# Triangular inversions of a decoder kernel: the value product on four corners of the array instead of two

## The chip, the cores and the metric

The kernel runs on one core of a Trainium2 chip. The core has TensorE (matrix products, PE in the profile, with its weight loads as PEld), VectorE (DVE), ScalarE (ACT), GpSimd (POOL) and SyncE (SP), which issues the transfers. The metric is the device time of one execution in microseconds (us); lower is better.

## The reference, cut to what matters

Two decoder layers over 256 tokens of width 1024. Each layer mixes three branches (RWKV-7, gated DeltaNet, sparse latent attention), adds a cross attention over 256 memory tokens, and ends in a feed-forward part (dense in layer 0, top 2 of 8 experts in layer 1). Two of the branches are recurrences over tokens that a chunked kernel turns into the inverse of a unit triangular matrix for each head and chunk of 64 tokens:

```python
    # gated DeltaNet, for each of 8 heads and 4 chunks of C = 64 tokens
    Lmat = jnp.where(strict, jnp.einsum('bhnid,bhnjd->bhnij', kb, k) * decay, 0.0)
    rhs = jnp.concatenate([v * beta, kb * jnp.exp(g)[..., None]], axis=-1)
    sol = lax.linalg.triangular_solve(Lmat + jnp.eye(C, dtype=jnp.float32), rhs,
                                      left_side=True, lower=True, unit_diagonal=True)
    ...
    # RWKV-7, for each of 16 heads, one token after another
    def step(S, inp):
        r_t, w_t, k_t, v_t, kk_t, a_t = inp
        sa = jnp.einsum('bhvk,bhk->bhv', S, -kk_t)
        S = (S * w_t[:, :, None, :] + sa[..., None] * (kk_t * a_t)[:, :, None, :]
             + v_t[..., None] * k_t[:, :, None, :])
        return S, jnp.einsum('bhvk,bhk->bhv', S, r_t)
```

All of this is computed in float32.

## The kernel before

Every engine has a program of its own, written as Python generators that are interleaved by hand; what an engine does next is fixed by the place of each `yield`, and the engines meet at semaphores (`wait_ge`, `then_inc`, and a `Counter` that keeps the numbers).

**The inversion.** `invert` (TensorE), and the two functions called `inverted` (one for ScalarE, one for VectorE) compute unit triangular inverses by doubling: 6 levels (`LEVELS`), block size 1, 2, 4 up to 32. One call treats two *sets*, i = 0 and 1; a set is eight 64x64 matrices, four (q = 0 to 3) on partitions 0 to 63 and four on partitions 64 to 127 (`HALF`). For each level and set:

- **F** (L765): TensorE adds 8 products of 64x64 by 64 columns into columns 0 to 255 of bank 2 + i. The last level has none.
- **W** (L2223): VectorE multiplies that bank with the mask of the next level into `w`, an operand of the next F and V.
- **V** (L770): TensorE adds 8 products of 64x64 by 128 columns (64 at the last level) into bank 4 + i, which then holds, side by side, the matrix and the inverse so far.
- **VU** (L1596): ScalarE copies the whole bank 4 + i (128x512) into `vu`, the other operand of the next F and V.

Every product of a matrix on partitions 0 to 63 also has its result on partitions 0 to 63, and in the same way for the other half: of the four 64x64 corners of the array, the two on the diagonal are used. A product in float32 stands in the profile as two LDWEIGHTS and two MATMUL rows, so 8 products are "x16". At the end of a call ScalarE copies the inverses to `xt_` (L1602). Ahead of the levels, TensorE writes F's start (L748), and V's start as a product with the identity (L753) and two with the corner identity (L755) for each set.

**What lies around it.** An inversion is called 12 times, 6 in each layer. `filled` on TensorE puts one *dense unit* (two products of 128x256 at L799, a quarter of a projection tile) behind each of the `yield`s in `invert`, and, where the yielded value is true, one step of a second generator. In this text the calls have letters:

- **B** (first and third in each layer, `rw_set(i, i)`): RWKV, beside the *front* of the next two pairs of heads (`front_rw`). The front is a chain over three engines: on TensorE two low-rank products (L859, L860), then two sums (L865, L867), then the Gram products (L875, L876); on ScalarE two copies and a square, four sigmoids and a table load (L1650 to L1665), later a logarithm and exponentials; on VectorE four stretches, the first (from L2248) ending at L2257, behind the sigmoids.
- **A** (second and fourth, `rw_set(i, 2 + i)`): RWKV, beside dense units alone.
- **G1** (fifth): gated DeltaNet with `corners` (it also joins the 64-blocks to 128), beside `front_gd` of four heads, three steps to a head. `both` advances this front at every yield.
- **G2** (sixth): the same, beside the first recurrence, `recur_gd(0)`, and dense units.

The order of each engine's queue is that of its own generators: what ScalarE and VectorE do for the front stands in line with VU and W.

Of the kernel before, what the change touches and what calls it, by code (L numbers as in the profile page):

```python
# [14 lines left out]
P = 128  # L15
# [130 lines left out]
def build(nc, x, mem, consts, params, w_in, w2, a2, v1, v2, w_uq, w_uk, w_uv, w_qI, w_mix, xa_q, xa_kv, xa_o,  # L146
          ff_g, ff_u, ff_d, router, me_g, me_u, me_d, final_norm, v_first, out):
    ctx = ExitStack()
    with ctx:
# [89 lines left out]
        HALF = (slice(0, 64), slice(64, P))  # L239

# [395 lines left out]
        def _(pe):  # L636
# [100 lines left out]
            def invert(sets, corners=None):  # L737
# [12 lines left out]
                for i, (nt, xt_, vu, w) in enumerate(sets):  # L750
                    if corners is not None:
                        pe.wait_ge(S["inv_VU"], c.need("inv_VU"))
                    mm(bk4(4 + i)[:, :, 64:P], C("ident"), b4(C("eye2")), start=True, stop=True, skip_group_check=True)  # L753
                    for h, p_ in enumerate(HALF):
                        m = mm(bk4(4 + i)[p_, :, 0:64], C("eye2")[p_], nt[h], start=False, stop=True, skip_group_check=True)  # L755
                    m.then_inc(S["inv_V"], 1)
                for b in range(LEVELS):
                    last = b == LEVELS - 1
                    for i, (nt, xt_, vu, w) in enumerate(sets):
                        pe.wait_ge(S["inv_W"], c.need("inv_W"))  # L760
# [771 lines left out]
        def _(act):  # L1532
# [52 lines left out]
            def inverted(sets, corners=False):  # L1585
# [6 lines left out]
                for b in range(LEVELS):  # L1592
                    for i, (nt, xt_, vu, w) in enumerate(sets):
                        act.wait_ge(S["inv_V"], c.need("inv_V"))
                        act.wait_ge(*c.last())
                        sc.activation(vu, bk4(4 + i), ACT.Copy).then_inc(*c.inc("inv_VU"))  # L1596
                        yield i
                for i, (nt, xt_, vu, w) in enumerate(sets):
                    act.wait_ge(S["inv_V"], c.need("inv_V"))
                    for h, p_ in enumerate(HALF):  # L1600
                        act.wait_ge(*c.last())
                        sc.activation(xt_[p_, :, p_], bk4(4 + i)[p_, :, 64:P], ACT.Copy).then_inc(*c.inc("inv_XT" if h else "act_step"))  # L1602
                if corners:
                    yield 0
                    for i in range(len(sets)):
                        act.wait_ge(S["inv_V"], c.need("inv_V"))
                        act.wait_ge(*c.last())
                        sc.activation(gB[0:64, i, 1], bk(4 + i, 0, T)[0:64].rearrange("p (a b) -> p a b", a=4), ACT.Copy).then_inc(*c.inc("inv_VU"))
                    yield 1
# [535 lines left out]
        def _(dve):  # L2145
# [72 lines left out]
            def inverted(sets, corners=False):  # L2218
                q4 = lambda ap: ap.rearrange("p (a b) -> p a b", a=4)
                for b in range(LEVELS):  # L2220
                    for i, (nt, xt_, vu, w) in enumerate(sets):
# [3 lines left out]
                        yield i  # L2225
# [637 lines left out]
```

## Time and profile before

| | |
|---|---|
| time, median of 3 runs | 2955.32 us (2954.4 to 2958.49) |
| span of the profiled execution | 2958.0 us |
| TensorE busy in it | 2588.5 us, 88% |
| ScalarE busy | 1469.3 us, 50% |
| VectorE busy | 1706.3 us, 58% |
| mean granted TensorE clock | 0.954 |
| the 12 inversion calls together | 561.67 us, TensorE busy 487.99 us |

The span runs from the first to the last instruction. No separate time is listed for the profiled execution; its span lies within the range of the three runs, 2.7 us above their median, so no time of note lies around it. Busy times are of each engine for itself and overlap. In the rows below a timeline row gives start, duration (from the start of the first to the end of the last of the merged instructions), engine, line, operation, tiles and count, and in brackets how long the engine had been idle and who ended that.

### The profile page before, as it was taken

To read this page: it belongs to the slowest core of one execution; us is meant where nothing else is said; L and a number is where in the kernel's file an instruction comes from. 1 tells how busy PE (TensorE), PEld (TensorE's weight loads), DVE (VectorE), ACT (ScalarE), POOL (GpSimd) and SP (SyncE) were. 2 spreads that over 40 slices of the span, in tenths; PEclk is the share of its full clock that TensorE was granted. 3 is DMA by queue.
4 is the path that set the end of the run, shared out by engine and by line. 5 is a ranking of instruction groups with operands and counts; after the bars stand their busy time and mean duration, and the time that the engine had idled before them with its cause. 6 is when DMAs were issued, how large, how long until landed. Compare 5 with 4: busy or idle time off the path is not lost.

```text
span 2958.0 us, 67158 instructions
## 1 busy us (share of the span) xinstructions
PE 2588.5 (88%) x29799; PEld 2117.4 (72%) x29818; DVE 1706.3 (58%) x1983; ACT 1469.3 (50%) x1911; POOL 358.2 (12%) x180
## 2 busy tenths in 40 slices
PE   7988988899797989897988999787898898998986
PEld 6766666777465768665666777557888888888875
DVE  2445463234215542545462233128999999999996
ACT  2233343233224331433343233137888889888885
POOL 0000001000000000000001000001323243324231
PEclk9999999999998999998989999898999999999999
DMA  6411120123216634301121133237999999999994
GB/s 201 135 41 47 31 86 29 37 93 114 95 62 228 202 119 139 100 30 31 58 63 32 58 107 100 100 125 289 388 386 386 386 386 388 382 386 390 385 387 183
DMA packets 304032, 531.34 MB, mean 180 GB/s; under 512 B 18528, under 2 KB 145760, under 8 KB 303360
## 3 DMA queue, kind: packets, MB, share of 16 engines
q1 hardware_dynamic: 303600, 525.99, 50.3%
q8 instruction: 236, 3.87, 0.5%
q10 hardware_dynamic: 144, 1.05, 0.1%
q14 instruction: 52, 0.43, 0.0%
HBM read 524.91 MB, written 2.10 MB: 178 GB/s over the span
## 4 chain that ended last, share of the span: by engine, by line
PE 53%; DVE 33%; ACT 7%; issue 6%; DMA 0%; ACTq 0%; DVEq 0%; SPq 0%
DVE arena L2713 24%; PE bank L799 11%; PE bank L700 9%; PE bank L770 4%; PE bank L1277 4%; PE bank L1236 4%; PE bank L765 3%; PE bank L718 2%; DVE yacc L2721 2%; PE bank L1293 2%; PE bank L644 2%; PE bank L1025 1%; ACT arena L1897 1%; PE bank L875 1%; PE bank L1030 1%
## 5 line engine op out<-in xcount | busy, mean ns | idle before, releaser
L2713 DVE TENSOR_TENSOR arena<-ring,arena 128x2048 bf16<-128x2048 f32 x336 | 833.4, 2525 | 3.8 <-ACT arena L2012 3.8
L2012 ACT ACTIVATE arena<-ring 128x2048 bf16<-128x2048 f32 x336 | 640.4, 1911 | 98.9 <-DMA ring<-in_moe_w_down 30.2
L1378 PE MATMUL bank<-arena 128*128 128x0 bf16 x10752 | 490.6, 209 | 99.4 <-DVE arena L2713 96.3
L1378 PEld LDWEIGHTS bank<-arena 128*128 128x128 bf16 x10752 | 478.6, 100 | 113.7 <-DVE arena L2713 105.3
L799 PE MATMUL bank<-feat,ring 128*128 128x256 f32 x1664 | 433.6, 399 | 8.4 <-ACT ring L1575 2.3
L1527 POOL TENSOR_TENSOR arena<-yacc,arena 128x512 bf16<-128x512 f32 x112 | 300.2, 2692 | 1004.5 <-ACT arena L2035 1004.5
L799 PEld LDWEIGHTS bank<-feat,ring 128*128 128x128 f32 x1664 | 308.6, 196 | 87.3 <-issue 43.1
L1395 PEld LDWEIGHTS bank<-arena 128*128 128x128 bf16 x5376 | 237.8, 98 | 23.0 <-issue 20.0
L1395 PE MATMUL bank<-arena 128*128 128x0 bf16 x5376 | 245.0, 206 | 7.3 <-issue 3.8
L700 PE MATMUL bank<-feat,ring 128*128 128x256 f32 x1056 | 236.8, 388 | 7.7 <-issue 5.7
L700 PEld LDWEIGHTS bank<-feat,ring 128*128 128x128 f32 x1056 | 205.7, 195 | 38.2 <-ACT feat L1566 8.9
L1504 POOL TENSOR_TENSOR arena<-arena 64x512 f32<-64x512 f32 x16 | 23.1, 1443 | 1152.1 <-ACT arena L1677 971.8
L1582 ACT ACTIVATE arena<-bank 128x256 f32<-128x256 f32 x120 | 46.1, 384 | 189.3 <-PE bank L700 91.2
L644 PE MATMUL bank<-cs,arena 128*128 128x128 f32 (+1 forms) x424 | 71.0, 304 | 69.3 <-ACT arena L1558 40.4
L1277 PE MATMUL bank<-arena 128*128 128x256 bf16 x1056 | 119.7, 276 | 10.6 <-DVE arena L2610 10.6
L2223 DVE TENSOR_TENSOR arena<-bank,cs 128x256 f32<-128x256 f32 x144 | 61.1, 424 | 117.5 <-PE bank L765 70.9
L1277 PEld LDWEIGHTS bank<-arena 128*128 128x128 bf16 x1056 | 104.5, 99 | 26.4 <-issue 11.0
L644 PEld LDWEIGHTS bank<-cs,arena 128*128 128x128 f32 (+1 forms) x424 | 53.8, 157 | 83.1 <-issue 29.2
L770 PE MATMUL bank<-arena 64*64 64x128 f32 (+1 forms) x1536 | 102.7, 276 | 6.6 <-ACT arena L1596 4.2
L765 PEld LDWEIGHTS bank<-arena 64*64 64x64 f32 x1280 | 47.4, 140 | 83.2 <-issue 43.6
L765 PE MATMUL bank<-arena 64*64 64x64 f32 x1280 | 56.4, 229 | 56.9 <-ACT arena L1596 32.5
L1582 ACT ACTIVATE ring<-bank 128x256 f32<-128x256 f32 x50 | 19.2, 384 | 153.4 <-PE bank L700 153.4
(355 smaller groups left out, 3434.5 us busy)
## 6 DMA issues: line engine op xcount, KB each, us to landing
ring<-in_moe_w_gate SPq DMA_DIRECT2D x112, 1024.0 KB, 8.4
ring<-in_moe_w_up SPq DMA_DIRECT2D x112, 1024.0 KB, 7.9
ring<-in_moe_w_down SPq DMA_DIRECT2D x112, 1024.0 KB, 8.4
ring<-in_w_in SPq DMA_DIRECT2D x76, 1024.0 KB, 5.2
ring<-in_xa_w_kv SPq DMA_DIRECT2D x16, 1024.0 KB, 5.3
ring<-in_ffn_w_gate SPq DMA_DIRECT2D x11, 1024.0 KB, 5.4
ring<-in_ffn_w_up SPq DMA_DIRECT2D x11, 1024.0 KB, 5.4
ring<-in_ffn_w_down SPq DMA_DIRECT2D x11, 1024.0 KB, 7.0
```

The lines of the kernel that those rows point to most:

```text
L644: return tr_(o, i_, C("ident")[0:i_.shape[0], 0:i_.shape[0]])
L700: m = mm(o, w[:, k, j * P:(j + 1) * P], src[:, k, :], start=k == 0, stop=k == kt - 1)
L765: m = mm(quarter(bk(2 + i), q)[p_], vu[p_, q, 0:64], w[p_, b % 2, 64 * q:64 * q + 64], start=False, stop=True, skip_group_check=True)
L770: m = mm(bk4(4 + i)[p_, q, f], w[p_, b % 2, 64 * q:64 * q + 64], vu[p_, q, f], start=False, stop=True, skip_group_check=True)
L799: m = mm(o, w[:, k, j * P:(j + 1) * P], src[:, k, :], start=k == 0, stop=k == KT - 1)
L1236: m = mm(bk(4 + 2 * h + t), src[:, 4 * half + k, t * P:(t + 1) * P], w[:, k, :], start=half == 0 and k == 0, stop=half == 1 and k == 3)
L1277: m = mm(bk(b, col, T), w[wi][:, k, j * P:(j + 1) * P], feat_parts[xi][:, k, :], start=n == 0 and k == 0, stop=n == 2 and k == KT - 1)
L1378: m = mm(o, w[k // 4][wi][:, k % 4, col:col + P], xg[:, e % 2, xi, k, :].shape_from_register(width[e % 2]), start=i == 0 and k == 0, stop= ...
L1395: m = mm(o, w[wi][:, j, d * P:(d + 1) * P], act_parts[xi][:, 2 * (pair % 4) + j, :].shape_from_register(width[e % 2]), start=f == 0 and h ...
L1527: nc.gpsimd.tensor_tensor(act_parts[1][:, pair, :], sil[:, q % 4], act_parts[0][:, pair, :], ALU.subtract).then_inc(S["mo_al"], 1)
L2012: sc.activation(w_parts[b][0], ring[:, b * FFN_SLOT:(b + 1) * FFN_SLOT], ACT.Copy).then_inc(S["w_hi"], 1)
L2713: v.tensor_tensor(w_parts[b][1], ring[:, b * FFN_SLOT:(b + 1) * FFN_SLOT], w_parts[b][0], ALU.subtract).then_inc(S["w_lo"], 1)
```

## The change

V's result is split. Of the four matrices q of a half, q = 0 and 1 stay as they were and go to columns 0 to 255 of bank 4 + i (`straight`); q = 2 and 3 now go to the **other** partition half, into columns 256 to 511 of bank 2 + i (`crossed`), whose first half holds F. The eight products of a V are issued in the order q = 0, 2, 1, 3, so that all four corners come in turn. The copy VU becomes three: one 128x256 of `straight`, and two 64x256 of `crossed`, one for each half, which bring the data back to its own partitions. The same is done for the copies to `xt_` (four of 64x128 a set instead of two of 64x256) and for V's start (twice as many products, of half the columns). ScalarE's wait for its own last instruction ahead of these copies is gone.

The order changes as well. Within a level TensorE now issues both F, yields, then both V, and yields. Since crossed V and F share a bank, V of level b waits for W of level b + 1 (before, F and V of a level both followed the wait for the W that they read); the first `crossed` start waits for the first W. ScalarE and VectorE yield at other places to match.

```diff
@@ -237,6 +237,15 @@
+        def inv_halves(i):
+
+            return (bk(4 + i, 0, T).rearrange("p (a b) -> p a b", a=2), bk(2 + i, T, T).rearrange("p (a b) -> p a b", a=2))
+
+        def inv_v(i, q, h):
+
+            straight, crossed = inv_halves(i)
+            return straight[HALF[h], q] if q < 2 else crossed[HALF[1 - h], q - 2]
@@ -750,26 +759,38 @@
-                    mm(bk4(4 + i)[:, :, 64:P], C("ident"), b4(C("eye2")), start=True, stop=True, skip_group_check=True)
+                    straight, _ = inv_halves(i)
+                    mm(straight[:, :, 64:P], C("ident"), b4(C("eye2"), 2), start=True, stop=True, skip_group_check=True)
                     for h, p_ in enumerate(HALF):
-                        m = mm(bk4(4 + i)[p_, :, 0:64], C("eye2")[p_], nt[h], start=False, stop=True, skip_group_check=True)
+                        mm(straight[p_, :, 0:64], C("eye2")[p_], nt[h][:, 0:2], start=False, stop=True, skip_group_check=True)
+                for i, (nt, xt_, vu, w) in enumerate(sets):
+                    _, crossed = inv_halves(i)
+
+                    pe.wait_ge(S["inv_W"], c.need("inv_W"))
...
                 for b in range(LEVELS):
                     last = b == LEVELS - 1
                     for i, (nt, xt_, vu, w) in enumerate(sets):
-                        pe.wait_ge(S["inv_W"], c.need("inv_W"))
                         pe.wait_ge(S["inv_VU"], c.need("inv_VU"))
                         if not last:
...
                             m.then_inc(S["inv_F"], 1)
-                        f = slice(64 * last, P)
-                        for q in range(4):
+                    yield 0
+                    f = slice(64 * last, P)
+                    for i, (nt, xt_, vu, w) in enumerate(sets):
+
+                        if not last:
+                            pe.wait_ge(S["inv_W"], c.need("inv_W"))
+                        for q in (0, 2, 1, 3):
                             for h, p_ in enumerate(HALF):
-                                m = mm(bk4(4 + i)[p_, q, f], w[p_, b % 2, 64 * q:64 * q + 64], vu[p_, q, f], start=False, stop=True, skip_group_check=True)
+                                m = mm(inv_v(i, q, h)[:, f], w[p_, b % 2, 64 * q:64 * q + 64], vu[p_, q, f], start=False, stop=True, skip_group_check=True)
                         m.then_inc(S["inv_V"], 1)
-                        yield i
+                    yield 1
@@ -1591,21 +1612,28 @@
                 for b in range(LEVELS):
                     for i, (nt, xt_, vu, w) in enumerate(sets):
+                        straight, crossed = inv_halves(i)
                         act.wait_ge(S["inv_V"], c.need("inv_V"))
-                        act.wait_ge(*c.last())
-                        sc.activation(vu, bk4(4 + i), ACT.Copy).then_inc(*c.inc("inv_VU"))
-                        yield i
+                        sc.activation(vu[:, 0:2], straight, ACT.Copy).then_inc(*c.inc("act_step"))
+                        for h, p_ in enumerate(HALF):
+                            sc.activation(vu[p_, 2:4], crossed[HALF[1 - h]], ACT.Copy).then_inc(*c.inc("inv_VU" if h else "act_step"))
+                    if b:
+                        yield 1
+                    yield 0
...
@@ -2222,7 +2250,8 @@
                         v.tensor_tensor(q4(w[:, b % 2, :]), q4(bk(2 + i, 0, T)), b4(C("level", 64 * b, 64 * b + 64)), ALU.mult).then_inc(*c.inc("inv_W"))
                         dve.wait_ge(*c.last())
-                        yield i
+                        if b or not corners:
+                            yield i if b else 0
```

In the changed file F is L781, V is L791, the dense unit L820, VU L1617 and L1619, W L2251.

**TensorE's program, one level in call A of layer 0**, before (bank 2 and 3 are F, 4 and 5 V, 7 the dense unit):

```order
L765 MATMUL bank2<-arena 64x64 x8
L770 MATMUL bank4<-arena 64x128 x8
L799 MATMUL bank7<-feat,ring 128x256 x2
L765 MATMUL bank3<-arena,yacc 64x64 x8
L770 MATMUL bank5<-yacc,arena 64x128 x8
L799 MATMUL bank7<-feat,ring 128x256 x2
```

and now:

```order
L781 MATMUL bank2<-arena 64x64 x8
L781 MATMUL bank3<-arena,yacc 64x64 x8
L820 MATMUL bank7<-feat,ring 128x256 x2
L791 MATMUL bank4<-arena 64x128 x2
L791 MATMUL bank2<-arena 64x128 x2
L791 MATMUL bank4<-arena 64x128 x2
L791 MATMUL bank2<-arena 64x128 x2
L791 MATMUL bank5<-yacc,arena 64x128 x2
L791 MATMUL bank3<-yacc,arena 64x128 x2
L791 MATMUL bank5<-yacc,arena 64x128 x2
L791 MATMUL bank3<-yacc,arena 64x128 x2
L820 MATMUL bank7<-feat,ring 128x256 x2
```

The two dense units of a level stay; the second F moved ahead of the first V, and the products of a V alternate between its two banks.

**ScalarE's program at the start of the first call B**, before (L1596 is VU of set 0 and set 1; L1575 empties a dense tile; L1650 on is the first piece of the front):

```order
L1596 ACTIVATE arena<-bank4 128x512
L1596 ACTIVATE yacc<-bank5 128x512
L1575 ACTIVATE ring<-bank7 128x256
L1650 ACTIVATE yacc<-arena 64x4x64
L1652 ACTIVATE yacc<-arena 64x4x64
L1657 ACTIVATE arena<-arena 128x512
```

and now:

```order
L1617 ACTIVATE arena<-bank4 128x256
L1619 ACTIVATE arena<-bank2 64x256 x2
L1617 ACTIVATE yacc<-bank5 128x256
L1619 ACTIVATE yacc<-bank3 64x256 x2
L1617 ACTIVATE arena<-bank4 128x256
L1619 ACTIVATE arena<-bank2 64x256 x2
L1617 ACTIVATE yacc<-bank5 128x256
L1619 ACTIVATE yacc<-bank3 64x256 x2
L1596 ACTIVATE ring<-bank7 128x256
L1678 ACTIVATE yacc<-arena 64x4x64
L1680 ACTIVATE yacc<-arena 64x4x64
L1685 ACTIVATE arena<-arena 128x512
```

The VU of the second level now stands ahead of the front's first piece; before it stood behind that piece and the table load.

**VectorE's program at the same place**, before (L2223 is W; L2248 to L2257 the front's first piece):

```order
L2223 TENSOR_TENSOR arena<-bank2,cs 128x256
L2223 TENSOR_TENSOR arena<-bank3,cs 128x256
L2248 TENSOR_SCALAR arena<-arena,par 128x256 x2
L2252 TENSOR_SCALAR arena<-arena,par 128x256 x2
L2254 SCALAR_TENSOR_TENSOR arena<-arena 128x512
L2257 SCALAR_TENSOR_TENSOR arena<-arena,par 128x256 x2
L2223 TENSOR_TENSOR arena<-bank2,cs 128x256
L2223 TENSOR_TENSOR arena<-bank3,cs 128x256
```

and now:

```order
L2251 TENSOR_TENSOR arena<-bank2,cs 128x256
L2251 TENSOR_TENSOR arena<-bank3,cs 128x256
L2251 TENSOR_TENSOR arena<-bank2,cs 128x256
L2251 TENSOR_TENSOR arena<-bank3,cs 128x256
L2277 TENSOR_SCALAR arena<-arena,par 128x256 x2
L2281 TENSOR_SCALAR arena<-arena,par 128x256 x2
L2283 SCALAR_TENSOR_TENSOR arena<-arena 128x512
L2286 SCALAR_TENSOR_TENSOR arena<-arena,par 128x256 x2
L2251 TENSOR_TENSOR arena<-bank2,cs 128x256
```

The second pair of W moved ahead of the front's first piece, and each later piece stands one level later as well.

## Rows read from the trace of the kernel before

**Rows 1.** The page, TensorE's busy time in the whole span.

```profile
PE 2588.5 (88%) x29799; PEld 2117.4 (72%) x29818; DVE 1706.3 (58%) x1983; ACT 1469.3 (50%) x1911; POOL 358.2 (12%) x180
```

**Rows 2.** Busy time by stretch: calls B, A, G1, G2 of layer 0; sum of all 12.

```profile
145.65:199.65 54.00, 43.55 (x505) 32.81 (x505) 21.04 (x36) 22.18 (x39) 2.88 (x2) 0.91 0.13 40
199.65:232.00 32.35, 32.35 (x450) 24.63 (x452) 15.93 (x36) 10.13 (x20) 0.00 (x0) 1.00 0.12 35
...
472.85:540.73 67.88, 55.34 (x561) 41.32 (x560) 18.29 (x44) 26.21 (x56) 8.56 (x12) 0.92 0.10 25
540.73:583.00 42.27, 39.01 (x505) 31.00 (x505) 9.24 (x18) 11.46 (x23) 0.00 (x0) 1.00 0.11 31
...
sum 561.67, PE 487.99 PEld 369.68 DVE 203.25 ACT 201.64 POOL 28.63; mean PE 40.67 PEld 30.81 DVE 16.94 ACT 16.80 POOL 2.39
```

**Rows 3.** Timeline in call A, one set of a level: F, V, dense unit, next F.

```profile
210.64 0.68 PE L765 MATMUL bank<-arena,yacc 64*64 64x64 f32 x16
211.15 1.04 PE L770 MATMUL bank<-yacc,arena 64*64 64x128 f32 x16
212.12 1.13 PE L799 MATMUL bank<-feat,ring 128*128 128x256 f32 x4
213.19 0.68 PE L765 MATMUL bank<-arena 64*64 64x64 f32 x16
```

**Rows 4.** Line L770 by itself: durations in ns min/median/max, span, forms.

```profile
L770 PE MATMUL bank<-arena x1536: 218/269/419, 149.5 to 1666.9; 64*64 64x128 f32 x160, 64*64 64x64 f32 x32
```

**Rows 5.** Timeline of the RWKV recurrence: products on two column tiles that share all rows.

```profile
236.13 0.69 PE L995 MATMUL bank<-arena 128*64 128x64 f32 x16
236.64 0.64 PE L1002 MATMUL bank<-arena 128*64 128x64 f32 x16
```

**Rows 6.** Timeline: ScalarE copies back to back without a wait, and four with one.

```profile
1987.56 1.91 ACT L2133 ACTIVATE arena<-feat 128x2048 bf16<-128x2048 f32 x1 [0.81 <-DVE feat L2183]
1989.38 3.69 ACT L2012 ACTIVATE arena<-ring 128x2048 bf16<-128x2048 f32 x2
...
197.92 1.67 ACT L1602 ACTIVATE arena<-bank 64x256 f32<-64x256 f32 x4
```

**Rows 7.** Timeline of V's start in call A: identity, corner identities, next set.

```profile
200.72 0.70 PE L753 MATMUL bank<-cs 128*128 128x256 f32 x2
201.35 0.65 PE L755 MATMUL bank<-arena,cs 64*64 64x256 f32 x4
201.93 0.70 PE L753 MATMUL bank<-cs 128*128 128x256 f32 x2
```

**Rows 8.** Timeline of call B: first long wait, VectorE's third piece of the front.

```profile
157.82 1.01 DVE L2257 SCALAR_TENSOR_TENSOR arena<-arena,par 128x256 f32<-128x256 f32 x2
158.86 0.88 DVE L2223 TENSOR_TENSOR arena<-bank,cs 128x256 f32<-128x256 f32 x2
159.34 1.12 PE L765 MATMUL bank<-arena 64*64 64x64 f32 x16 [4.11 <-DVE arena L2223]
...
169.89 1.42 DVE L2270 TENSOR_TENSOR arena<-arena 128x512 f32<-128x512 f32 x1
...
177.33 0.37 DVE L2287 COPY arena<-arena 128x4 f32<-128x4 f32 x2
```

**Rows 9.** What TensorE waited for in that call: total us, times, longest.

```profile
PE bank L765 <- DVE arena L2223: 4.7, 2, 4.1
PE bank L765 <- ACT arena L1596: 3.8, 1, 3.8
```

**Rows 10.** Timeline of one head's front in G1, and that head's stretch.

```profile
495.25 0.69 ACT L1812 ACTIVATE arena<-bank,small 128x512 f32<-128x512 f32 x1 [0.67 <-PE bank L1025]
...
497.43 0.60 ACT L1596 ACTIVATE arena<-bank 128x512 f32<-128x512 f32 x1
...
498.18 0.68 PE L765 MATMUL bank<-arena 64*64 64x64 f32 x16 [2.10 <-ACT arena L1596]
...
491.54:505.32 13.78, 10.89 (x121) 8.12 (x122) 4.16 (x10) 5.88 (x13) 2.14 (x3) 1.00 0.01 1
```

More of the change, by code:

```diff
@@ L752, in invert @@
                         pe.wait_ge(S["inv_VU"], c.need("inv_VU"))
-                    mm(bk4(4 + i)[:, :, 64:P], C("ident"), b4(C("eye2")), start=True, stop=True, skip_group_check=True)
+                    straight, _ = inv_halves(i)
+                    mm(straight[:, :, 64:P], C("ident"), b4(C("eye2"), 2), start=True, stop=True, skip_group_check=True)
                     for h, p_ in enumerate(HALF):
-                        m = mm(bk4(4 + i)[p_, :, 0:64], C("eye2")[p_], nt[h], start=False, stop=True, skip_group_check=True)
+                        mm(straight[p_, :, 0:64], C("eye2")[p_], nt[h][:, 0:2], start=False, stop=True, skip_group_check=True)
+                for i, (nt, xt_, vu, w) in enumerate(sets):
+                    _, crossed = inv_halves(i)
+                    pe.wait_ge(S["inv_W"], c.need("inv_W"))
+                    mm(crossed[:, :, 64:P], C("ident"), b4(C("eye2"), 2), start=False, stop=True, skip_group_check=True)
+                    for h, p_ in enumerate(HALF):
+                        m = mm(crossed[HALF[1 - h], :, 0:64], C("eye2")[p_], nt[h][:, 2:4], start=False, stop=True, skip_group_check=True)
                     m.then_inc(S["inv_V"], 1)
@@ L1593, in inverted @@
                     for i, (nt, xt_, vu, w) in enumerate(sets):
+                        straight, crossed = inv_halves(i)
                         act.wait_ge(S["inv_V"], c.need("inv_V"))
-                        act.wait_ge(*c.last())
-                        sc.activation(vu, bk4(4 + i), ACT.Copy).then_inc(*c.inc("inv_VU"))
-                        yield i
+                        sc.activation(vu[:, 0:2], straight, ACT.Copy).then_inc(*c.inc("act_step"))
+                        for h, p_ in enumerate(HALF):
+                            sc.activation(vu[p_, 2:4], crossed[HALF[1 - h]], ACT.Copy).then_inc(*c.inc("inv_VU" if h else "act_step"))
+                    if b:
+                        yield 1
+                    yield 0
                 for i, (nt, xt_, vu, w) in enumerate(sets):
                     act.wait_ge(S["inv_V"], c.need("inv_V"))
+                    straight, crossed = inv_halves(i)
                     for h, p_ in enumerate(HALF):
-                        act.wait_ge(*c.last())
-                        sc.activation(xt_[p_, :, p_], bk4(4 + i)[p_, :, 64:P], ACT.Copy).then_inc(*c.inc("inv_XT" if h else "act_step"))
+                        sc.activation(xt_[p_, 0:2, p_], straight[p_, :, 64:P], ACT.Copy).then_inc(*c.inc("act_step"))
+                    for h, p_ in enumerate(HALF):
+                        sc.activation(xt_[p_, 2:4, p_], crossed[HALF[1 - h], :, 64:P], ACT.Copy).then_inc(*c.inc("inv_XT" if h else "act_step"))
+                yield 1
                 if corners:
-                    yield 0
                     for i in range(len(sets)):
@@ L1608, in inverted @@
                         sc.activation(gB[0:64, i, 1], bk(4 + i, 0, T)[0:64].rearrange("p (a b) -> p a b", a=4), ACT.Copy).then_inc(*c.inc("inv_VU"))
+                    yield 0
                     yield 1
```

## The prediction, made before the changed kernel had run

> **What bounds the kernel now.** I read the page first: TensorE is busy 88% of the span [rows 1], so the question is whether the inversions are TensorE's time too. The stretches say so: the twelve calls take 561.67 us, 19% of the span, with TensorE busy 487.99 of them; call A is filled by TensorE alone (32.35 of 32.35), while B, G1 and G2 leave it idle 10.4, 12.5 and 3.3 us [rows 2]. Transfers are no matter there (the DMA share, second last column, is 0.13 or less).
>
> The timeline of A gives one set of one level: F starts at 210.64, V 0.51 later, the dense unit 0.97 after V, the next F 1.07 after that; 2.55 us in all, 5.10 a level [rows 3]. What sets V's 0.97? Its last row ends 1.04 after its first began, and one row lasts 0.269 [rows 3, 4], so 16 rows start over 0.77 us, 51 ns apart. F, with half the columns, gives (0.68 - 0.22) / 15 = 31 ns; a row of F lasts about 0.22. So V goes by its columns on two corners, not by how fast products can be issued. The half-width V of a last level is at that lower distance already.
>
> **Part 1: V on four corners.** No row of before has four corners at work for long. The nearest: F and a product of 128x64 on two column tiles, which share all rows of the array, also starts every 31 ns ((0.69 - 0.22) / 15) [rows 5], where one after the other its 64 columns would take what V's 128 take on two corners, 51. So column tiles do run beside each other on the same rows, and F shows that row halves do. I take 27 to 31 ns for V's rows on four corners; the bounds are 26 (half of V's distance) and 51 (nothing won). V then costs 16 x 0.027 = 0.43 to 16 x 0.031 = 0.50 in place of 16 x 0.051 = 0.82. I take 0.38 saved. There are 12 calls x 2 sets x 5 full-width levels = 120 of them: 46 us of TensorE's time at full clock.
> The Trainium skill ("TensorE: Matmul & The Clock Gate", what overlaps and what doesn't) says that a weight load overlaps a running product only when its row group differs. By that rule the third product of a V, on the rows of the first, would wait for it, V would stay at 0.82, and this part would bring 0 rather than 46. The trace disagrees for column tiles, as far as the 31 ns go.
>
> **Part 2: V's start.** Before, a set costs 0.63 (identity) and 0.58 (corners), 1.21, of which 0.43 each is streaming and 0.20 and 0.15 the change of tile shape [rows 7]. Now there are four halves of 0.21 + 0.20 + 0.21 + 0.15 = 0.77: 3.1 us against 2.4. Behind it the first F waits for ScalarE's larger copies, some 0.6 us more. Together +1.3 us a call.
>
> **Part 3: three copies for one.** VU took 0.60 [rows 10]. Four copies of 64x256, each waiting for the last, take 1.67 [rows 6], 0.42 apiece. Without that wait, two long copies take 3.69 where one takes 1.91, so the second starts 0.13 before the first is done [rows 6]. Three short ones are then 3 x 0.42 = 1.25 with waits and 1.25 - 2 x 0.17 = 0.9 at best, where overlap and wait both go; I take 0.95.
> The Trainium skill ("ScalarE: Activation LUTs", what a table load costs) has back-to-back activations overlap by 93 ns; by that figure an estimate is 1.25 - 2 x 0.09 = 1.07, and A's level would be 0.2 longer. The trace's 0.13 lies a little above the page's figure.
>
> In A a level now runs: both V 0.88, change 0.15, dense 0.85, change 0.21, both F 0.88, change 0.15, dense 0.85, change 0.21: 4.2 us. Against it stands ScalarE: set 0's result is there 0.73 after its V began, then 0.95 and 0.9 of copies, so VU of set 1 comes at 2.6, where TensorE wants it at 2.5; and VectorE: W, a convolution step of some 1.0, W behind F hold V of set 1 for about 0.1. I take 4.4 against 5.10: 0.7 x 5 levels = 3.5, less 1.3 for the start and some 0.4 for the first level and the last copies: **A: -1.8**. With 1.2 us of copies a level is 4.9 and A gains nothing; with 27 ns and no wait it is 4.2 and A gains 2.5.
>
> **Part 4: the order, where waits end.** In B, TensorE stands 4.1 us for W, which VectorE makes only behind the front's first piece (done at 158.83), and later 3.8 us for VU, which stands on ScalarE behind the front's exponentials and a table load [rows 8, 9]. Now VU and W of the second level stand ahead of that piece, so this F goes at once. The stall doesn't vanish: V of the same level waits for the W of the next, which is behind the piece. What is late: the piece itself, since its sigmoids now queue behind two sets of copies, 1.9 us. I reckon from the front's two low-rank products, 0.6 later than before: copies, the piece's copies and square, four sigmoids, VectorE's 2.5 and W, then V at about 161.9. By then TensorE has done one F pair and a dense unit more than before, and waited about 4.0. The 3.8 us wait for VU goes, and in its place V of the fourth level waits some 3.8 us for a W behind VectorE's third piece, which lasts from 169.89 to 177.7 [rows 8]. The last levels lose their 0.6 us waits and one of the waits at the end. So idle time falls from 10.4 to some 8.5 (-2), V saves 5 x 2 x 0.38 = 3.8, the start costs 1.3: **B: -4.7**, bounds 0 and -8. Both long waits drop the clock: after the 4.11 us idle the same F takes 1.12 instead of 0.68 [rows 8, 3], at the lower of the clock's two levels, and I expect the same after the new ones, no better.
>
> In G1 a head's front takes 13.78 us, TensorE busy 10.89 [rows 10]. The wait of 2.10 is for a VU that stands on ScalarE behind the front's logarithm and exponentials (from 495.25) [rows 10]. Now the copies stand ahead of them, so F doesn't wait; what is late next is the next head's square, behind the copies, for which the sum L1025 will wait 1.2 to 1.6 us in every second head. Three levels now serve two heads. A head then costs 10.9 - 3 x 0.38 = 9.75 plus 0.9 idle, 10.7, which is 3.1 less; I take 2.6, because ScalarE's queue is fuller than I can follow, times four heads, less 1.3: **G1: -9**, bounds -4 and -13. **G2**: 10 V save 3.8, the start costs 1.3, 3.3 us of waits turn over without clear sign, ahead of five levels like A's: -3, bounds 0 and -5.
>
> **The sum.** B and A occur four times, G1 and G2 twice: 4 x -4.7, 4 x -1.8, 2 x -9, 2 x -3 is -19, -7, -18, -6, **-50 us**. Against the profiled 2958.0 this is 2908; the runs' median is 2.7 below, so **2905**. What follows is TensorE's or waits for TensorE, and the experts' transfers start from buffers that TensorE frees, so the gain moves through to the end.
>
> **The rivals.**
> *A V that is no faster.* Corners on the same rows take turns: the third product's weights wait until the first has streamed its 128 columns. V 0.82, A's level 5.0 and with the dearer start A 0; B -1, G1 -4, G2 0. That is -12: 2943. For it: no row has four corners busy. Against: the 31 ns of [rows 5]. 0.12. (It is what the Trainium skill's rule, cited in part 1, would do here.)
> *V's new wait eats the order's gain.* W sits behind the front's pieces on VectorE; if TensorE stands as long as before and falls to the lower clock as often, B gives -1.5, G1 -4, A and G2 as forecast: -27, 2928. For it: VectorE already holds the longest wait [rows 9]; against it, in G1 the long wait is ScalarE's [rows 10]. 0.18.
> *The waits close entirely.* B -8, G1 -13, A -2.5, G2 -5: -78, 2877. 0.08.
> *ScalarE becomes the bound, and it is slower.* A's level on ScalarE's path is 2.5 us plus twice a set's copies, so it passes 5.10 when three copies cost over 1.3; a copy across the halves would have to take over 0.55 for that. No row has a copy from one half to the other. At 0.7 each, three cost 1.8, A's level is 6.1: +6.3 a call; with +2 in B, +4 in G1 and +4 in G2 that is 4 x 6.3 + 4 x 2 + 16 = +49. Between the threshold and this, +20: 2975. 0.07.
> *No effect in the end.* Start, copies and queues cancel the V: 2955. 0.03.
> The forecast itself: 0.52, by itself 2888 to 2922.
>
> **How the numbers follow.** The range of 2880 to 2943 leaves out the slower rival, no effect, half of the closed waits and a tail of the serial corners, under 2 in 10. Faster by over 0.2% (6 us, what a measurement of this kernel tells from no change): the forecast, the closed waits, the eaten order, and nearly all of the serial corners: 0.88. Slower 0.08, same 0.04.
>
> **What the profile after would show.** V (L791) x16 from first start to last end 0.68 to 0.75 in A rather than 1.04: part 1 right; 1.04 still: the serial rival. Three copies from start to end under 1.0, and none of 64x256 above 0.4: part 3. A's stretch at 30.4. In B, no F waiting for L1617 or L1619, and two waits of about 4 us ahead of V (L791) for L2251; if they are 5 or more, the order's rival. In G1 the sum over a head's squares (L1046) waits for the square, and a head takes 10 to 11 us. What makes it wrong most easily: ScalarE's queue in G1 and B, where I followed the chain, and the clock after each idle stretch.

## The result, and the profile after

The changed kernel takes 2974.44 us in the median of four runs (2969.13 to 2976.64), the kernel before 2954.86 beside it (2950.37 to 2958.49): 1.006 times as long, with an interval of 1.0045 to 1.0074. It is slower by some 20 us, where 50 fewer were forecast and the range ended at 2943.

The page says little at first: TensorE's busy time fell as meant, ScalarE's rose by 86 us [rows 1].

```profile
PE 2551.6 (86%) x29954; PEld 2075.0 (70%) x29962; DVE 1700.9 (57%) x1983; ACT 1555.3 (52%) x2247; POOL 361.6 (12%) x180
```

The stretches of layer 0's calls B, A, G1 and G2 (length, busy time by engine, granted clock third from last) stand against [rows 2]:

```profile
145.90:198.06 52.16, 39.52 (x517) 28.35 (x517) 20.13 (x36) 29.37 (x67) 2.54 (x2) 0.91 0.14 42
198.06:246.06 48.00, 38.05 (x457) 27.46 (x456) 15.94 (x36) 17.03 (x48) 0.00 (x0) 0.78 0.07 23
496.22:554.22 58.00, 50.56 (x573) 35.87 (x573) 18.29 (x44) 33.20 (x84) 8.55 (x12) 0.94 0.12 29
554.22:595.13 40.91, 35.56 (x513) 27.50 (x512) 9.24 (x18) 18.65 (x51) 0.00 (x0) 1.00 0.14 41
```

B, G1 and G2 are shorter. A, which TensorE alone filled before, is 48 us for 32, TensorE idle for 10 of them, the granted clock 0.78 for 1.00. Over all twelve calls (first two lines of the table in the next section) that is +45 us in A and -25 in the others, +20 together, which is the difference of the two times.

One level of A and the start of the next, ScalarE and TensorE by time:

```profile
209.53 0.67 PE L791 MATMUL bank<-arena 64*64 64x128 f32 x16
210.01 0.62 PE L791 MATMUL bank<-yacc,arena 64*64 64x128 f32 x16
210.26 0.38 ACT L1617 ACTIVATE arena<-bank 128x256 f32<-128x256 f32 x1 [3.61 <-PE bank L791]
210.67 0.78 ACT L1619 ACTIVATE arena<-bank 64x256 f32<-64x256 f32 x2
211.47 0.38 ACT L1617 ACTIVATE yacc<-bank 128x256 f32<-128x256 f32 x1
211.88 0.78 ACT L1619 ACTIVATE yacc<-bank 64x256 f32<-64x256 f32 x2
212.76 0.38 ACT L1596 ACTIVATE ring<-bank 128x256 f32<-128x256 f32 x1
213.19 2.08 PE L820 MATMUL bank<-feat,ring 128*128 128x256 f32 x4 [2.56 <-ACT ring L1596]
215.20 1.12 PE L781 MATMUL bank<-arena 64*64 64x64 f32 x16
```

V is fast: 0.67 and 0.62 a set against 1.04 [rows 3]. Then come six copies in 2.4 us. Only behind them ScalarE empties the dense unit's bank (L1596), and the next dense unit (L820) waits 2.56 us for it; F, which has its VU by then, stands behind that unit on TensorE. The dense unit then takes 2.08 us for 1.13 and F 1.12 for 0.68: the granted clock is at the lower level (1.2 GHz) after the idle time. V starts at 209.53, 219.11, 224.13, 231.06, 235.92 and 242.99: every second level, in which a dense tile ends, takes 6.9 to 9.6 us, the others 4.9 to 5.0, less than before's 5.10. Of what TensorE waited for in the whole kernel (total, times, longest) this comes second:

```profile
PE bank L820 <- ACT ring L1596: 41.6, 22, 2.8
```

In the same view of before the dense units stood 2.3 us for that copy (L1575 there), in 5 places.

### The profile page after: what moved, and what is told of

Its sections match the earlier page's. It is cut to its first block, busy times and chain, and to the rows that moved or that the text cites. A ratio compares the mean times of both kernels' runs of the same rounds, so it can differ in the third digit from the quotient of the medians.

```text
span 2967.0 us, 67493 instructions
## 1 busy us (share of the span) xinstructions
PE 2551.6 (86%) x29954; PEld 2075.0 (70%) x29962; DVE 1700.9 (57%) x1983; ACT 1555.3 (52%) x2247; POOL 361.6 (12%) x180
## 4 chain that ended last, share of the span: by engine, by line
PE 49%; DVE 32%; ACT 12%; issue 7%; DMA 0%; ACTq 0%; DVEq 0%; SPq 0%
DVE arena L2742 23%; PE bank L820 11%; PE bank L709 9%; PE bank L1298 4%; PE bank L1257 4%; PE bank L727 2%; PE bank L1314 2%; ACT arena L1619 2%; DVE yacc L2750 2%; PE bank L653 2%; PE bank L781 2%; PE bank L791 2%; ACT yacc L1619 1%; ACT arena L1617 1%; PE bank L1046 1%
## 5 line engine op out<-in xcount | busy, mean ns | idle before, releaser
L2742 DVE TENSOR_TENSOR arena<-ring,arena 128x2048 bf16<-128x2048 f32 x336 | 832.2, 2521 | 3.8 <-ACT arena L2040 3.8
L820 PE MATMUL bank<-feat,ring 128*128 128x256 f32 x1664 | 438.4, 404 | 62.1 <-ACT ring L1596 41.6
L820 PEld LDWEIGHTS bank<-feat,ring 128*128 128x128 f32 x1664 | 313.8, 199 | 142.1 <-issue 62.2
L2251 DVE TENSOR_TENSOR arena<-bank,cs 128x256 f32<-128x256 f32 x144 | 61.1, 424 | 210.1 <-PE bank L781 150.5
L1617 ACT ACTIVATE arena<-bank 128x256 f32<-128x256 f32 x96 | 36.8, 383 | 212.6 <-PE bank L791 158.5
L1603 ACT ACTIVATE arena<-bank 128x256 f32<-128x256 f32 x120 | 46.1, 384 | 181.9 <-PE bank L709 86.3
L2332 DVE TENSOR_TENSOR arena<-ring 128x256 f32<-128x256 f32 x50 | 21.3, 426 | 127.3 <-ACT ring L1603 127.3
L2639 DVE TENSOR_TENSOR arena<-ring,arena 128x2048 bf16<-128x2048 f32 x33 | 74.5, 2289 | 11.8 <-ACT arena L2013 11.8
```

Of the source, the lines that this page charges most:

```text
L820: m = mm(o, w[:, k, j * P:(j + 1) * P], src[:, k, :], start=k == 0, stop=k == KT - 1)
L2639: v.tensor_tensor(w_parts[b][1], ring[:, b * FFN_SLOT:(b + 1) * FFN_SLOT], w_parts[b][0], ALU.subtract).then_inc(*c.inc("w_lo"))
L2742: v.tensor_tensor(w_parts[b][1], ring[:, b * FFN_SLOT:(b + 1) * FFN_SLOT], w_parts[b][0], ALU.subtract).then_inc(S["w_lo"], 1)
```

## The experiments

For each kernel, the length of the calls in its profiled run, summed over the four B, four A, two G1 and two G2 (from a call's first product to the next call's first, or to the last copy of its result), and the time. The ratio is to the kernel before as it was timed beside each of them (2954.9 to 2957.2 us).

```
kernel                                       B      A     G1    G2   all 12    time   ratio to before, interval
before                                   213.2  129.6  132.8  83.8   559.4  2954.9
the changed kernel                       207.1  174.6  116.0  81.8   579.5  2974.4   1.0045-1.0074
1  emptied ahead in A                    210.3  140.5  115.6  83.3   549.7  2942.2   0.9930-0.9967
2  emptied ahead in A and B              200.5  140.5  115.9  81.8   538.7  2929.6   0.9885-0.9918
3  before's code in A                    205.7  133.2  117.5  81.8   538.2  2932.2   0.9906-0.9939
4  order without corners                 196.1  144.2  106.5  81.3   528.2  2920.0   0.9856-0.9889
5  old order and corners in A            209.3  115.5  117.4  81.8   524.1  2915.9   0.9839-0.9872
6  4, with before's code in A            197.1  131.3  106.5  81.3   516.3  2906.8   0.9814-0.9847
7  4, emptied ahead in A and B           193.9  131.6  106.6  81.3   513.4  2909.2   0.9819-0.9852
8  7, V not waiting for W                165.3  130.2  106.2  80.1   481.7  2880.5   0.9720-0.9753
9  8, with 5's A                         165.2  113.3  106.1  80.1   464.8  2863.6   0.9670-0.9702
10 7, copy in three pieces               199.9  135.9  112.7  82.2   530.7  2927.2   0.9888-0.9921
11 8, corners in A's new order           165.2  133.7  106.2  80.1   485.1  2878.1   0.9740-0.9750
```

The lengths are those of one execution each: B, whose code is the same in the changed kernel and in experiments 1, 3 and 5, comes to 205.7 to 210.3, and G1 to 115.6 to 117.5. Differences below that spread are not read.

**Experiment 1: the dense bank emptied ahead of the copies, in A.** `behind` runs the dense unit's ScalarE turn one turn late, `filled` at once.

```diff
-    behind(inverted([rw_set(i, 2 + i) for i in range(2)]), None, side, WITH_INVERT[g])
+    filled(inverted([rw_set(i, 2 + i) for i in range(2)]), None, side, WITH_INVERT[g])
```

> The changed kernel, with one word altered in stage A (the inversion beside dense units alone): ScalarE takes the dense unit's turn at once instead of one turn late, so that the copy that empties the dense tile's bank stands ahead of the six V copies where it stood behind them. Theory 1 (the loss in A is TensorE waiting for that bank, 2.56 to 2.65 us at every second level, and the lower clock that follows): the waits of the dense products for L1596 go in A, its levels come down to the 4.9 us that a level without the wait has now, its four calls from 48.0, 40.9, 44.9 and 40.8 us to 31 to 34 each, and the time from 2974 to 2936 to 2945. Theory 2 (the order F F, V V with 2.4 us of copies between them is itself too long for A, and the bank wait only takes idle time that would be there anyway): A stays above 40 us a call and the time above 2965.

2942.2 us, and A's four calls 35.8, 34.8, 34.9 and 34.9. In the rows the emptying copy now stands ahead of V's copies, and the dense unit follows V at once:

```profile
207.82 0.39 ACT L1596 ACTIVATE ring<-bank 128x256 f32<-128x256 f32 x1 [1.83 <-PE bank L820]
208.20 0.62 PE L791 MATMUL bank<-yacc,arena 64*64 64x128 f32 x16
208.45 0.38 ACT L1617 ACTIVATE arena<-bank 128x256 f32<-128x256 f32 x1 [0.24 <-PE bank L791]
208.75 1.13 PE L820 MATMUL bank<-feat,ring 128*128 128x256 f32 x4
...
210.91 0.68 PE L781 MATMUL bank<-arena,yacc 64*64 64x64 f32 x16 [0.41 <-ACT yacc L1619]
```

And the call's stretch:

```profile
198.56:234.36 35.80, 30.86 (x457) 22.55 (x456) 15.93 (x36) 17.03 (x47) 0.00 (x0) 0.95 0.10 31
```

The clock is back at 0.95 and the level at 4.87 throughout (V at 207.71, 212.58, 217.44). The place of one copy, with no instruction more or fewer, takes 34 of A's 45 us away: theory 1 holds. The calls are still 1 to 2 us over the 31 to 34 that it gave, and some 3 over before's 32. The longer start is in them (the first F comes 6.27 us after the call begins, for 3.39 before, with the clock at its lower level at first) and a last wait of 1.12 us for the copies.

**Experiment 2: the same in B.** There the dense turn also goes ahead of the front's step (a helper `ahead`, which runs the side first, then the other).

> As the kernel before this one, and in stage B too the dense unit's turn is taken at once on ScalarE (ahead of the front's step of that turn). Theory 1: the waits of B's dense products for L1596 (1.59, 2.56 us and their like, some 5.7 us in the first call) go as well; each of the four B calls is 1 to 3 us shorter than 52, and the time is 4 to 10 us below that of the kernel with A alone. If B is set by its V products waiting for VectorE behind the front's work instead, B stays at 51 to 52 and the two kernels agree within 3 us.

2929.6 us, 12.6 below the kernel with A alone, a little more than expected; B's calls are 49.6, 49.4, 52.0 and 49.6. The waits for L1596 (4.2 us) are gone from B's first call, but V's waits for the masking W grow there from 3.4 us in one place to 6.7 in two, 4.6 the longest. B had both, and a part of the first turned into the second.

**Experiment 3: before's code in A alone.**

> The changed kernel with stage A's four calls in the code of the kernel before (V on two corners, one copy a set, F and V of a set together), and the rest changed. If the whole loss sits in A, its calls are back at 32 to 33 us, and the time is 2974 less 45, 2926 to 2934, with B and G at the values of the changed kernel (sums 207, 116 and 82 us). If part of the 45 us was time that A took over from work that must be done later anyway, less comes back and the time is over 2940.

2932.2 us, A 33.9, 33.9, 32.7 and 32.8. So the loss sat in A: some 42 us come back where 45 were in the calls. Experiments 1 and 3 together: most of A's loss is what queues behind the six copies, and 7 us are left between their A (140.5 and 133.2). Those 7 are not the order's: without corners and with the bank emptied ahead, A is 131.6 (experiment 7).

**Experiment 4: the order without the corners.** V straight in its own bank and one copy a set, everywhere; the order of F and V, and V's wait for W, as in the changed kernel.

```diff
-    m = mm(inv_v(i, q, h)[:, f], w[...], vu[p_, q, f], ...)
+    m = mm(bk4(4 + i)[p_, q, f], w[...], vu[p_, q, f], ...)
...
-    sc.activation(vu[:, 0:2], straight, ACT.Copy)...
-    for h, p_ in enumerate(HALF):
-        sc.activation(vu[p_, 2:4], crossed[HALF[1 - h]], ACT.Copy)...
+    sc.activation(vu, bk4(4 + i), ACT.Copy)...
```

> The changed kernel's order (both sets' F, then both sets' V, V waiting for W) with V straight on two corners in bank 4+i and one 128x512 copy a set, everywhere: the order alone, without corners. V is 1.04 instead of 0.65 a set, the copies 1.2 instead of 2.4 us a level. If the gain in G1 (58.0 against 67.9 and 64.9) is the order's, G1 stays at 57 to 61; if it is the corners', it goes back to 64 to 68. By theory 1 the wait for the dense tile's bank in A shrinks with the copies, from 2.6 to about 1.4 us, and A comes down by 4 to 8 us a call in spite of the slower V: the time is 2945 to 2960. If the corners carry the gain, it is 2975 to 2990.

2920.0 us, far below what either theory gave. The order alone is worth 37 us against before (2957.2 beside it); the corners, which were to be the bulk of the gain, cost 54 on top of it (2974.4 against 2920.0; -11 in B, -30 in A, -9.5 in G1 in the calls when they go). G1, half of whose gain I had put down to the faster V, is 53.3 a call without it, 58.0 with it. In A the order alone costs 15 us (144.2 for 129.6), with the dense units standing 3.6 us for L1589, the emptying copy, in the first call, where the changed kernel has 7.8: two copies of 0.6 stand ahead of it now, not six pieces in 2.4. One level of G1, V of both sets in 1.96 us:

```profile
483.91 1.96 PE L784 MATMUL bank<-arena 64*64 64x128 f32 x32
485.15 0.58 ACT L1609 ACTIVATE arena<-bank 128x512 f32<-128x512 f32 x1
485.80 1.13 PE L813 MATMUL bank<-feat,ring 128*128 128x256 f32 x4
485.92 0.60 ACT L1609 ACTIVATE arena<-bank 128x512 f32<-128x512 f32 x1 [0.19 <-PE bank L784]
486.86 1.15 PE L774 MATMUL bank<-arena 64*64 64x64 f32 x32
```

Set 0's copy runs beside set 1's V, and set 1's beside the dense unit; both F follow without a wait. With the corners V needs 1.10 us for both and the copies 2.4, so that F stands 0.30 and 0.53 for them behind the same dense unit:

```profile
505.81 1.10 PE L791 MATMUL bank<-arena 64*64 64x128 f32 x32
506.85 1.13 PE L820 MATMUL bank<-feat,ring 128*128 128x256 f32 x4
...
508.28 0.68 PE L781 MATMUL bank<-arena 64*64 64x64 f32 x16 [0.30 <-ACT arena L1619]
...
509.50 0.68 PE L781 MATMUL bank<-arena 64*64 64x64 f32 x16 [0.53 <-ACT arena L1619]
```

From the first V to the end of the second F that is 4.10 us without corners and 4.37 with them, though V itself is 0.86 shorter.

**Experiment 5: corners in the old order, in A.** F, V and a dense unit for one set, then for the other; the crossed half in banks 0 and 1, which A doesn't use, so that no product of V shares a bank with what VectorE reads.

> The changed kernel, but stage A in the order of the kernel before (F, V, dense for one set, then for the other) with V on four corners: its crossed half lies in the free banks 0 and 1 instead of the upper half of F's bank, so that V need not wait for W. In this order a set's three copies (1.19 us) lie beside the other set's F and V and a dense unit. Theory 1 (corners pay where the copies are covered): A's level is what TensorE works in it, 5.10 less 2 x 0.4 = 4.3 us, A 27.5 to 29.5 us a call against 32.7 to 33.9 with before's code in A, and the time 2912 to 2920. Theory 2 (the 2.4 us of copies a level, with the dense tile's emptying among them, bound A in any order, or the clock falls with the lesser load): A 31 to 36 us, the time 2930 to 2945.

2915.9 us, A 28.3, 29.4, 28.4 and 29.4, TensorE busy 27.71 of 28.30 us. A level is 4.23 us (207.72 to 211.95). The last two rows of F and the first two of V interleave and stand in rows of their own, so each has 14 here:

```profile
207.61 0.78 ACT L1715 ACTIVATE yacc<-bank 64x256 f32<-64x256 f32 x2
207.72 0.62 PE L848 MATMUL bank<-arena 64*64 64x64 f32 x14
208.24 0.61 PE L854 MATMUL bank<-arena 64*64 64x128 f32 x14
208.77 1.13 PE L883 MATMUL bank<-feat,ring 128*128 128x256 f32 x4
209.84 0.62 PE L848 MATMUL bank<-arena,yacc 64*64 64x64 f32 x14
...
211.95 0.62 PE L848 MATMUL bank<-arena 64*64 64x64 f32 x14
```

So the corners do pay, 16 us over experiment 3, and A is 14 us shorter than before. They need the copies under other work: here each set's 1.2 us lies beside the other set's F, V and dense unit.

**Experiment 6: the order without corners, before's code in A.**

> The order without corners, with stage A in the code of the kernel before. A goes from 35.4 to 37.0 us a call to 32 to 34, which is 8 to 14 us in all: 2906 to 2913. This is the order's gain in B and G alone, without corners and without A's bank wait.

2906.8 us, as expected: -16 in B, -26 in G1, -2.5 in G2 against before.

**Experiments 7 and 8: emptied ahead, and then V's wait for W taken away.** Experiment 7 is 4 with the dense turns of experiment 2. In experiment 8 V, which has a bank of its own there, doesn't wait for the masking that reads F's bank; the wait stands ahead of the next F. The wait for W ahead of V's start goes with it.

```diff
     for i, (nt, xt_, vu, w) in enumerate(sets):
+        pe.wait_ge(S["inv_W"], c.need("inv_W"))
         pe.wait_ge(S["inv_VU"], c.need("inv_VU"))
...
     for i, (nt, xt_, vu, w) in enumerate(sets):
-        if not last:
-            pe.wait_ge(S["inv_W"], c.need("inv_W"))
         for q in (0, 2, 1, 3):
```

> The order without corners everywhere, and the dense unit's turn taken at once on ScalarE in A and B. The bank waits of A (1.17 and 1.26 us at every second level) and of B go: A's level is 5.10 us throughout (its TensorE work: 1.31 F, 2.13 V, two dense units), A 32.5 to 34 us a call, B 1 to 2 us less than 48.3 to 49.9; the time 2903 to 2912. If the wait is only exchanged for one on W or on the copies, over 2915.

> As the kernel before this one, and the wait for W stands ahead of the next level's F, where it stood ahead of V (V lies in a bank of its own here, so VectorE may still read F's bank beside it). If V's wait for W costs time (my rival b: V waits 19.0 us in 8 places for the masking, behind the front's work in B), B is 1 to 4 us a call shorter and the time 5 to 12 us less than with the wait. If the next F waits for W instead (the masking is late either way), the two agree within 3 us. A level in G then is bound by V, copy, F: 5.0 us or less against 5.3 now, or the same if VectorE is in the loop by W for F anyway.

2909.2 us for the first, A's level 5.10 (V at 201.90, 206.99, 212.08), as expected. The second takes 2880.5 us: 29 less, more than twice what I gave for it, and B's four calls are 41.5, 41.2, 41.5 and 41.2 for 49.0, 47.8, 49.2 and 47.8. The same V in B's first call, and the call's stretch; first with the wait, then without:

```profile
160.26 1.01 DVE L2282 SCALAR_TENSOR_TENSOR arena<-arena,par 128x256 f32<-128x256 f32 x2
161.30 0.88 DVE L2247 TENSOR_TENSOR arena<-bank,cs 128x256 f32<-128x256 f32 x2
161.78 1.97 PE L793 MATMUL bank<-arena 64*64 64x128 f32 x16 [3.21 <-DVE arena L2247]
163.54 1.91 PE L793 MATMUL bank<-yacc,arena 64*64 64x128 f32 x16
```

```profile
146.20:195.23 49.03, 42.00 (x504) 32.12 (x504) 20.34 (x36) 22.11 (x39) 3.08 (x2) 0.93 0.14 44
```

```profile
156.83 1.09 PE L791 MATMUL bank<-arena 64*64 64x128 f32 x16
157.75 1.04 PE L791 MATMUL bank<-yacc,arena 64*64 64x128 f32 x16
158.72 1.13 PE L886 MATMUL bank<-arena,cs 128*128 128x512 f32 x2
...
161.57 0.68 PE L783 MATMUL bank<-arena 64*64 64x64 f32 x16
```

```profile
144.60:186.10 41.50, 39.16 (x506) 30.05 (x506) 20.53 (x36) 21.92 (x39) 2.89 (x2) 1.00 0.17 52
```

With the wait, V stands 3.21 us for a masking behind the front's piece on VectorE, and then runs at half the clock (1.97 for 1.09). Without it V, the front's sums and a dense unit fill that time, the F behind them finds its W made, and the granted clock of the whole call is 1.00. In the whole kernel V stood for W in 8 places of experiment 7:

```profile
PE bank L793 <- DVE arena L2247: 21.1, 8, 3.2
```

The wait isn't moved on: in experiment 8 no wait of TensorE for W is left. The gain of 29 is more than these 21.1 us; the clock that no longer falls behind them (0.93 to 1.00 in the first call) is the rest that the trace shows.

**Experiment 9: the best of both.** Experiment 8 in B and G, experiment 5's A.

> The kernel of the last experiment (order without corners, dense tile emptied ahead, V not waiting for W) in B and G, and in A the old order with corners in the free banks. Both parts act in stages of their own, so their gains should add: A from 32.5 to 28.3 to 29.5 us a call, 13 to 16 us in all, the time 2864 to 2870. If A's gain is given back by the clock behind it (TensorE is less loaded with corners) or by the matmuls behind A meeting a later load, it is 2870 to 2880.

2863.6 us, 3.1% below before (0.967 to 0.970). The gains add: A 113.3, 17 less than in experiment 8 where 13 to 16 were forecast, and the rest as there.

**Experiment 10: the copy in three pieces, without corners.** Experiment 7 with the one 128x512 copy cut into 128x256 and twice 64x256, all from the set's own bank.

> The order without corners, with the dense tile emptied ahead (2909.2), and ScalarE's one 128x512 copy of a set cut into the three pieces of the changed kernel (128x256 and twice 64x256), from the same bank: the corners' copies without the corners. If the pieces cost as there (1.19 against 0.60 us a set), G1's level is the chain V, copies, F: it goes from 53.3 to 59 to 63 us a call, B and A gain nothing and lose 0 to 3 us a call, and the time is 2925 to 2945; the corners' faster V is then what brings the corner version (2929.6) back to or below it. If the pieces from one and the same bank overlap, so that the corner version's cost lies in its banks, it is 2909 to 2915.

2927.2 us, 18 more than in one piece. The first two pieces overlap a little in one bank; the second starts 0.28 after the first:

```profile
214.57 0.38 ACT L1618 ACTIVATE arena<-bank 128x256 f32<-128x256 f32 x1 [0.65 <-PE bank L793]
214.85 0.77 ACT L1620 ACTIVATE arena<-bank 64x256 f32<-64x256 f32 x2
215.64 0.39 ACT L1618 ACTIVATE yacc<-bank 128x256 f32<-128x256 f32 x1
```

A set starts 1.07 after the one before it, against 1.21 in the changed kernel. G1 comes out at 56.4 a call on average, under the 59 to 63 expected. Against this kernel the corner version of experiment 2 (2929.6) is no faster, within their spread: with the copies in pieces, a V 0.4 us shorter, its split start and its eight last copies bring nothing together. Of the 20 us that the corners cost with the bank emptied ahead (2929.6 against experiment 7's 2909.2), the pieces alone are 18.

**Experiment 11: corners in A in the new order**, with banks 0 and 1, beside experiment 8.

> As the first kernel of this group, but A in the new order with corners in the free banks 0 and 1, V not waiting for W, the dense tile emptied at once. A's level is TensorE's work of 4.3 us if both sets' copies (2.4 us from the end of set 0's V) are covered by set 1's V and the dense unit (1.8 us) and set 0's F (0.7): A 28.5 to 30 us a call and the time 2864 to 2874, no different from the old order there. If set 1's F waits for its copies, the level is 4.4 to 4.9 us, A 30 to 33 us, the time 2872 to 2884: then the corners pay in the old order only.

2878.1 us and A 33.4 a call, where the old order had 28: the second case, and a little past its 33. Set 1's F waits for its copies, and a level is 4.95. Against experiment 8, which has no corners, A is 3.5 us longer in all and the time the same within the spread (2878.1 and 2880.5). From experiment 9 it differs in A's order and in the emptying turn that goes with it.

```profile
200.80 0.62 PE L857 MATMUL bank<-yacc,arena 64*64 64x128 f32 x16
202.26 0.38 ACT L1710 ACTIVATE yacc<-bank 128x256 f32<-128x256 f32 x1
202.67 0.78 ACT L1712 ACTIVATE yacc<-bank 64x256 f32<-64x256 f32 x2
203.59 0.68 PE L848 MATMUL bank<-arena,yacc 64*64 64x64 f32 x16 [0.50 <-ACT yacc L1712]
```

## Why the prediction was wrong, step by step

**Part 1** was right, at the good end of its 27 to 31 ns: the 16 rows of a full-width V take 0.67 or 0.62 us, from 1.04, and 0.67 is 27 ns from row to row by the same reckoning. The Trainium skill's rule ("TensorE: Matmul & The Clock Gate", what overlaps and what doesn't), as part 1 read it, gives 1.04 here; these rows disagree with it, and the rival that rested on it falls.

**Part 2** was right: the start's four halves begin 0.78 apart (146.98, 147.76, 148.54 in B's first call) where 0.77 was forecast. The first F comes 4.79 us after that call begins, for 3.40 before: 1.4 more, where 1.3 was forecast.

**Part 3** was the first miss. I took 0.95 us for three copies, from long copies that overlapped by 0.13. They start 0.41 apart where one lasts 0.38, and take 1.19. At that value my own working said that A's level is 4.9 and that A gains nothing; the level without a bank wait is 4.87. The overlap of 93 ns that the Trainium skill states ("ScalarE: Activation LUTs", what a table load costs) is not there between these pieces either; in experiment 10 it is, between the first two (0.10).

**The step that failed** is the working of A's level: "both V 0.88, change 0.15, dense 0.85, ... 4.2 us. Against it stands ScalarE". I set TensorE's work against the two sets' copies, and left out, put at nothing without a reason, the third thing in ScalarE's queue: the copy that empties the one bank of the dense unit. Before, it stood between two single copies, with a set's F and V to cover it. After, it stands behind six, and the dense unit it holds up stands ahead of F. A, forecast at -7 us for four calls, came out at +45, of which 34 go with that copy's place alone (experiment 1). With that copy late, the order by itself is +15 (experiment 4), and order and corners together are the +45. With the wait went the clock: 0.78 for 1.00 in the first call.

**B**, forecast at -19, came to -6, and **G1**, forecast at -18, to -17, **G2**, at -6, to -2. G1's number was right by luck: I had booked three shorter V a head, half of its gain. The order alone gives -26, and the corners take 9.5 of it back, since VU's copies are on the path there. The wait that I forecast for the sums of the squares (L1046) did come, 14.0 us in 10 places. In B the dense bank's waits (1.59 and 2.56 us in the first call) were missed too; experiment 2 takes 7 to 10 us from B by them (200.5 against 207.1 in the changed kernel and 210.3 in experiment 1).

**The rivals.** "ScalarE becomes the bound" gave 2975, and 2974 was measured, with 0.07 on it. The number is a coincidence, for its mechanism isn't what happened: it wanted three copies over 1.3 us, and they take 1.19; without the misplaced copy the level is below 5.10. "V's new wait eats the order's gain" was true at the same time and under-priced: I gave it 23 us (-27 in place of -50). The changed kernel's V stands for W in ten places:

```profile
PE bank L791 <- DVE arena L2251: 21.4, 10, 4.6
```

Experiment 8 finds 29 us for that wait, its clock with it, in a kernel where V has a bank of its own. The changed kernel can't give it up as it stands, since its crossed half lies in F's bank, which VectorE reads; that is a hidden price of the corners, measured only without corners here. The crossed half in another bank was not tried in B and G, so what corners would give there without that wait is open.

## What to carry to other kernels

When an edit makes an engine's turn longer, list everything that this engine does in the turn, and who waits for each item, the single-buffered side work above all; here the time went with the first item behind the longer block. Work that was split to make TensorE faster paid here only where its copies lay under other work of TensorE: in A the same corners gave -17 us in the old order (experiment 9 against 8) and +3.5 in the new one (11 against 8), and +30 in the new one while the dense bank was emptied late (the changed kernel against 4). And before a value shares a bank with another, price the wait that this forces at the engine that has the longest queue.

## What the runs showed of the hardware

- Four corners of the array work at once. In the single rows of the V at 211.15 before, the products start in pairs 7 ns apart, a pair every 109 ns. In the V at 209.53 of the changed kernel they start in fours 7 ns apart, and from the second four on again one every 109 ns: 27 ns a row for 51. The half-width V (64 columns) took 0.40 to 0.46 us for its 16 rows at full clock, against 0.68.
- Copies of 128x256 and 64x256 out of two different banks don't overlap (0.41 from start to start, 0.38 long); out of one bank the second started 0.28 after the first. The two pieces of 64x256 don't overlap in one bank either (0.77 for both, 0.37 long), so the bank alone doesn't decide it. No run here tells the bank from the crossing of the halves, or from the partition that a copy begins on.
- One idle stretch of 2.56 us of TensorE was followed by a dense unit at 2.08 for 1.13: the stretch from V at 209.53 to the next V is at a granted clock of 0.66, the level after it at 0.96. Two levels later 2.65 us of idle time were followed by a dense unit at full clock, so the length of the wait alone doesn't say what it costs. Ahead of the first, the clock had been at its lower level until shortly before (0.52 from 204.0 to 209.5).

```profile
209.53:219.11 9.58, 7.02 (x74) 5.00 (x73) 2.49 (x6) 2.67 (x7) 0.00 (x0) 0.66 0.01 2
219.11:224.13 5.02, 4.60 (x73) 3.46 (x73) 2.00 (x6) 2.28 (x6) 0.00 (x0) 0.96 0.00 0
...
227.89 1.10 PE L820 MATMUL bank<-feat,ring 128*128 128x256 f32 x4 [2.65 <-ACT ring L1596]
```
